# A four-layer hybrid encoder on one core: the first round of each MLP in a new order

## The chip, the cores and the metric

The kernel runs on one core of a Trainium2 chip. The metric is the device time of one execution in microseconds (us), the median of several runs. Five engines work side by side and wait for each other by semaphores: PE (TensorE, matmuls), ACT (ScalarE), DVE (VectorE), POOL (GpSimd) and SP (SyncE, which here issues the loads of weights).

## The reference

Four layers over 512 tokens of width 1024. Each layer adds a token mixer (latent attention, a gated recurrence, or windowed attention) and then an MLP:

```
x = x + mixer(rmsnorm(x, norm_mix[i]))
x = x + square(relu(rmsnorm(x, norm_mlp[i]) @ w1[i])) @ w2[i]      # 1024 -> 4096 -> 1024
```

with rmsnorm(x, g) = x * rsqrt(mean(x*x) + 1e-6) * g, and one more rmsnorm at the end. All in float32. The change is in the MLPs, of which there are four.

## The kernel before

**Precision.** Every float32 operand is split in two parts, a rounded high part and the remainder, and a product is three matmuls: high by high, low by high, high by low (L674 to L676). ACT rounds (a copy into w_hi, h_hi or u_hi), DVE subtracts (w_lo, h_lo, u_lo). `split(n)` on ACT (L2400) and on DVE (L1479) does this for the next n weight units of 128x1024. There are four slots for split weights, so ACT may round unit n when PE has done with unit n - 4.

**The MLP.** It runs in four slices of 1024 of the 4096 hidden features. A slice has two groups (g = 0, 1) of 512 features, and then the down projection of the slice, `down(0)` and `down(1)`: 8 units of 24 matmuls with 512 columns. A group is one round of `seven_products`: a fast matrix product of 2x2 blocks with seven block products (24 matmuls of 256 columns each) in place of eight. Its weights are sums of blocks of w1, in this order:

- product 1: A11; product 2: A11+A21; product 3: A11+A21+A22; product 4: A12; product 5: A21+A22; product 6: A22; product 7: A11+A12+A21+A22.

DVE makes each sum in place, just after its w_lo of an earlier unit (L1485, L1489, L1492, L1496). L1496 makes the weights of product 7; ACT's rounding of them waits for it by `sums_made`. On the other side stand the token halves H11, H21, H22 and their sums T1 to T4, which are made once per MLP in b11, b12, b21, b22; these four lie in the places that the second half of u_hi and u_lo takes later.

**One round on the other engines.** Between the products ACT and DVE combine results in c11, c21, c12, c22 (the buffer called relu): ACT copies a bank after product 1 (c11, L2527; product 3 waits for this copy), after product 3 (c21, L2536; product 5 waits) and the other bank (c22, L2539; product 6 waits). DVE adds after product 4 (L1707), subtracts after product 5 (c22, L1711; product 7 waits for this by `c_added`) and after product 6 (c21, L1714). Then ACT takes relu, squares and rounds (u_hi, L2518), DVE makes u_lo (L1687). A round of group 1 finds the results of group 0 still in c12 and c22: `u_lo_of(0, 1)` on DVE must be done before ACT overwrites c22.

**The first group of each MLP** is done differently, by plain products of four units (`square_group`), whose last quarter follows the two matmuls of `norm_sums` (L758, L760). It needs no sums of tokens, and while it runs ACT and DVE make T1 to T4. Its result stands in two PSUM areas. ACT takes the relu of area 0, then of area 1 (L2465), both into the buffer relu, DVE squares (L1611), ACT rounds (L2471), DVE makes the remainder (L1617). The c11 of the first round overwrites area 0's part of that buffer. Between these stand the root of the norm on ACT (a table load and L2447) and var on DVE (L1547). Down waits for both remainders by `u_ready`.

Each engine does its list in the order in which it is written; nothing is reordered.

Of the kernel before, what the change touches and what calls it, by code (L numbers as in the profile page):

```python
# [22 lines left out]
ALU = mybir.AluOpType  # L23
# [9 lines left out]
KC = D // P  # L33
# [119 lines left out]
def weight_plan():  # L153

    raws, ops, raw_starts = [], [], []
    sums = 0
# [110 lines left out]
def trunk(nc, A):  # L267
    raws, ops, raw_starts = weight_plan()
    with ExitStack() as ctx:
# [1175 lines left out]
        def _(dve):  # L1445
# [16 lines left out]
            def split(n):  # L1462

                for _ in range(n):
# [78 lines left out]
            def norm_var():  # L1543

                sum_ready()
                root_ready()
# [59 lines left out]
            def squares_of(q):  # L1606

                c.add(f"area{q}")
                dve.wait_ge(area_free[q], c.now(f"area{q}"))
                r = chunk(mlp_m["relu"], 2 * q, 2)  # L1610
                nc.vector.tensor_tensor(r, r, r, ALU.mult).then_inc(squared, 1)  # L1611

            def low_of_squares(q):

                c.add("u_hi")
                dve.wait_ge(u_hi_done, c.now("u_hi"))
                nc.vector.tensor_tensor(chunk(u_lo, 2 * q, 2), chunk(mlp_m["relu"], 2 * q, 2),  # L1617
                                        exact(chunk(u_hi, 2 * q, 2)), ALU.subtract).then_inc(u_ready, 1)

            def add_scaled(g):  # L1620

# [68 lines left out]
            def seven_products(g):  # L1690
# [3 lines left out]
                c.add("rounds")  # L1694
                c.add("tensor_unit", 3)
                split(1)
                if r % 7 == 0:
                    nc.vector.tensor_tensor(b21, b21, b11, ALU.add).then_inc(turned_made, 1)
                split(1)
                if r % 7 == 0:  # L1700
                    turned_lo(T4, b21)
                elif g == 1:
                    u_lo_of(0, 1)
                split(1)
                product_passed()
# [12 lines left out]
                split(1)  # L1718
                c.add(f"area{xy}")

            def mlp(gain):
# [14 lines left out]
                squares_of(0)  # L1736
                split(1)
                low_of_squares(0)
                norm_var()
                squares_of(1)  # L1740
                split(1)
                low_of_squares(1)
                c.add("psum_done")
                c.add("tensor_unit", 4)
                for s in range(SLICES):
                    if s:
                        seven_products(0)
                    seven_products(1)
# [620 lines left out]
        def _(act):  # L2369
# [89 lines left out]
            def relu_of(q):  # L2459

                if q == 0:
                    act.wait_ge(psum_done, c.now("psum_done") + 2)
                else:
                    units_passed(4)
                nc.scalar.activation(chunk(mlp_m["relu"], 2 * q, 2), area(q), ACT.Relu).then_inc(area_free[q], 1)  # L2465

            def high_of_squares(q):

                c.add("squared")
                act.wait_ge(squared, c.now("squared"))  # L2470
                nc.scalar.activation(chunk(u_hi, 2 * q, 2), chunk(mlp_m["relu"], 2 * q, 2), ACT.Copy  # L2471
                                     ).then_inc(u_hi_done, 1)

            def down_passed():
# [45 lines left out]
            def seven_products(g):  # L2520
# [8 lines left out]
                if r % 7 == 0:  # L2529
                    turned_hi(T4, b21)  # L2530
                elif g == 1:
                    u_hi_of(0, 1)
                split(1)
                product_passed()
# [17 lines left out]
                act.wait_ge(area_free[xy], jobs["round", r][0])  # L2552
                c.add("u_ready", 2)

            def half_gained(n, ks):

                for k in ks:
# [2 lines left out]
                                         ).then_inc(gained_done, 1)  # L2560

            def mlp(n, gain):
                half_gained(n - 1, range(4 if PHASES[n - 1][0] == "mla" else 0, KC))
                split(1)
                turned_hi(T1, b11)
                sums_hi()
# [12 lines left out]
                for s in range(SLICES):  # L2579
                    if s:  # L2580
                        seven_products(0)
                    seven_products(1)
                    u_hi_of(1, 1)
                    if s + 1 == SLICES:
                        break
# [641 lines left out]
```

## Time and profile before

| | us |
|---|---|
| median of 3 runs | 2027.55 (2026.84 to 2027.86) |
| profiled execution: its time | 2027.66 |
| profiled execution: its span, first to last instruction | 2025.8 |
| PE busy / DVE busy / ACT busy | 2000.3 / 1432.3 / 1063.8 |
| granted clock of PE, mean | 0.997 |

PE is busy for 99% of the span, so the time is what PE has to do, plus the stretches in which PE waits or runs at a lower clock. The time of an execution lies 1.9 us above its span. The timeline gives, for each instruction, its start and its duration; where instructions of an engine overlap in its pipeline the distance of two starts is what one costs. In brackets behind a row stands the idle time before it and what ended it.

### The profile page before, as it was taken

What the parts mean: (1) busy time and instruction counts of PE and PEld (TensorE: products, weight loads), DVE (VectorE), ACT (ScalarE), POOL (GpSimd) and SP (SyncE); (2) the same over time, 40 slices, a digit from 0 to 9 for tenths busy, and PEclk for the clock granted to TensorE, in tenths of its full rate; (3) what the DMA queues carried; (4) which work ended last, traced back from release to release, by engine and by line L of the source; (5) the groups of instructions that cost most, each with busy time, mean ns of one, the idle gap of its engine ahead of it and who ended that gap; (6) DMA issues with size and microseconds to landing.
All of it is one profiled execution on the core that took longest, in us unless ns stands there. A gap on an engine that the chain in (4) does not pass through costs nothing.

```text
span 2025.8 us, 28746 instructions
## 1 busy us (share of the span) xinstructions
PE 2000.3 (99%) x11760; PEld 1748.8 (86%) x11760; DVE 1432.3 (71%) x1682; ACT 1063.8 (53%) x1508; POOL 247.3 (12%) x323
## 2 busy tenths in 40 slices
PE   9999999999999999999999999999999999999998
PEld 8888898989878789899888888898988888899897
DVE  7866865756897867567698786675787758667574
ACT  6655534625466646254456663553647646353453
POOL 7002000000200200002731200000641011000000
PEclk9999999999999999999999999999999999999999
DMA  6222324314223133241332242422422223242431
GB/s 193 61 68 78 120 64 125 113 57 143 86 81 103 64 125 115 61 148 57 119 89 70 61 138 84 125 84 83 148 76 71 59 67 122 66 146 63 125 115 42
DMA packets 152595, 193.20 MB, mean 95 GB/s; under 512 B 17712, under 2 KB 95088, under 8 KB 152464
## 3 DMA queue, kind: packets, MB, share of 16 engines
q1 hardware_dynamic: 145520, 186.04, 29.6%
q0 software_dynamic: 4544, 3.94, 0.7%
q8 instruction: 93, 1.52, 0.3%
q10 hardware_dynamic: 2400, 1.38, 0.2%
q14 instruction: 38, 0.31, 0.1%
HBM read 185.30 MB, written 2.10 MB: 93 GB/s over the span
## 4 chain that ended last, share of the span: by engine, by line
PE 89%; DVE 6%; POOL 2%; ACT 2%; DMA 1%; issue 1%; ACTq 0%; DVEq 0%; POOLq 0%; SPq 0%
PE psum L674 27%; PE psum L676 27%; PE psum L675 27%; DVE h_lo L1514 2%; PE psum L1113 2%; PE psum L1086 1%; DVE w_lo L1479 1%; DMA arena<-in_mlp_w 1%; PE psum L1221 1%; DVE arena_r L1675 1%; PE psum L1062 1%; PE psum L1058 1%; PE psum L1057 1%; PE psum L1063 0%; DVE arena L1611 0%
## 5 line engine op out<-in xcount | busy, mean ns | idle before, releaser
L1479 DVE TENSOR_TENSOR w_lo<-w_raw,w_hi 128x1024 fp32r<-128x1024 f32 (+1 forms) x303 | 374.5, 1240 | 239.5 <-ACT w_hi L2400 238.3
L2400 ACT ACTIVATE w_hi<-w_raw 128x1024 fp32r<-128x1024 f32 (+1 forms) x307 | 323.6, 1060 | 328.3 <-PE psum L676 292.7
L674 PE MATMUL psum<-u_hi,w_hi 128*128 128x512 f32 x1256 | 492.2, 392 | 0.1
L676 PE MATMUL psum<-u_hi,w_lo 128*128 128x512 f32 x1256 | 489.1, 389 | 0.0
L675 PE MATMUL psum<-u_lo,w_hi 128*128 128x512 f32 x1256 | 489.1, 389 | 0.0
L674 PE MATMUL psum<-h_hi,w_hi 128*128 128x256 f32 (+1 forms) x1368 | 440.4, 322 | 0.0
L675 PE MATMUL psum<-h_lo,w_hi 128*128 128x256 f32 (+1 forms) x1368 | 437.5, 320 | 0.0
L676 PE MATMUL psum<-h_hi,w_lo 128*128 128x256 f32 (+1 forms) x1368 | 437.3, 320 | 0.0
L676 PEld LDWEIGHTS psum<-u_hi,w_lo 128*128 128x128 f32 x1256 | 235.8, 188 | 49.6
L674 PEld LDWEIGHTS psum<-u_hi,w_hi 128*128 128x128 f32 x1256 | 235.9, 188 | 49.0 <-DVE u_lo L1809 1.2
L674 PEld LDWEIGHTS psum<-h_hi,w_hi 128*128 128x128 f32 x1368 | 260.3, 190 | 20.2 <-issue 1.1
L2400 ACT ACTIVATE w_hi<-arena 128x1024 fp32r<-128x1024 f32 x120 | 127.1, 1060 | 286.5 <-PE psum L676 256.2
L675 PEld LDWEIGHTS psum<-h_lo,w_hi 128*128 128x128 f32 x1368 | 260.6, 190 | 19.3 <-issue 1.0
L675 PEld LDWEIGHTS psum<-u_lo,w_hi 128*128 128x128 f32 x1256 | 236.0, 188 | 47.4
L676 PEld LDWEIGHTS psum<-h_hi,w_lo 128*128 128x128 f32 x1368 | 260.5, 190 | 18.9
L1479 DVE TENSOR_TENSOR w_lo<-arena,w_hi 128x1024 fp32r<-128x1024 f32 x120 | 146.9, 1224 | 166.6 <-ACT w_hi L2400 166.2
L674 PE MATMUL psum<-arena_r,w_hi 128*128 128x256 f32 x672 | 191.0, 284 | 12.0 <-ACT arena L2527 11.0
L676 PE MATMUL psum<-arena_r,w_lo 128*128 128x256 f32 x672 | 190.8, 284 | 0.0
L675 PE MATMUL psum<-arena_r,w_hi 128*128 128x256 f32 x672 | 188.9, 281 | 0.0
L3067 POOL TENSOR_TENSOR ssq<-ssq,sq 128x512 f32<-128x512 f32 x49 | 80.2, 1636 | 685.4 <-ACT sq L2436 683.2
L674 PEld LDWEIGHTS psum<-arena_r,w_hi 128*128 128x128 f32 x672 | 128.6, 191 | 13.1 <-ACT arena L2527 11.8
L675 PEld LDWEIGHTS psum<-arena_r,w_hi 128*128 128x128 f32 x672 | 128.7, 191 | 0.0
(333 smaller groups left out, 2589.3 us busy)
## 6 DMA issues: line engine op xcount, KB each, us to landing
w_raw<-in_mlp_w SPq DMA_DIRECT2D x176, 512.0 KB, 3.9
arena<-in_mlp_w SPq DMA_DIRECT2D x80, 512.0 KB, 4.9
w_raw<-in_mla_w_o SPq DMA_DIRECT2D x16, 512.0 KB, 3.8
w_raw<-in_lru_w_in SPq DMA_DIRECT2D x16, 512.0 KB, 3.9
w_raw<-in_swa_w_in SPq DMA_DIRECT2D x12, 512.0 KB, 4.2
w_raw<-in_mla_w_ukv SPq DMA_DIRECT2D x8, 512.0 KB, 4.7
w_raw<-in_lru_w_out SPq DMA_DIRECT2D x8, 512.0 KB, 3.6
w_raw<-in_swa_w_o SPq DMA_DIRECT2D x8, 512.0 KB, 4.0
```

The source lines that it names most:

```text
L674: nc.tensor.matmul(out, stat[0], mov[0], start=start, stop=False, skip_group_check=skip)
L675: nc.tensor.matmul(out, stat[0], mov[1], start=False, stop=False, skip_group_check=skip)
L676: return nc.tensor.matmul(out, stat[1], mov[0], start=False, stop=stop, skip_group_check=skip)
L1057: nc.tensor.matmul(out, qh, KLO[s][:, 0:keys_n], start=False, stop=False)
L1058: nc.tensor.matmul(out, ql, KHI[s][:, 0:keys_n], start=False, stop=False)
L1062: nc.tensor.matmul(out, ROPE_Q[s][:, q_at], ROPE_KHI[:, 0:keys_n], start=False, stop=False)
L1086: mm = nc.tensor.transpose(area(a)[:, at:at + P], mla_m["p"][:, S_OFF[b] + P * jt:S_OFF[b] + P * (jt + 1)], ident)
L1113: mm = nc.tensor.matmul(bank(3, 1)[:, P * jt:T], mla_m["v"][:, v_at:v_at + VD], mla_m["pt"][:, T_OFF[jt]:T_OFF[jt] + n], start=jt == 0, st ...
L1479: ins = nc.vector.tensor_tensor(w_lo[:, to], tile, exact(w_hi[:, to]), ALU.subtract)
L1514: nc.vector.scalar_tensor_tensor(out=low, in0=rows, scalar=col(*gain(k)), in1=exact(high), op0=ALU.mult, op1=ALU.subtract).then_inc(h_read ...
L2400: nc.scalar.activation(w_hi[:, to], raw_tile(op.raw), ACT.Copy).then_inc(w_hi_done, 1)
L3067: g.tensor_tensor(to, to, source, ALU.add).then_inc(squares_added, 1)
```

## The change

1. In `weight_plan` and DVE's `split`, the sum for product 7 is made behind the w_lo of A22 (product 6) in place of the w_lo of A21+A22 (product 5). This holds for all 28 rounds.
2. The relu and squares of area 1 of the first group go to the place of b12 in place of the buffer relu, so the first round's c-buffers wait for area 0's part alone; ACT waits there for T3 (`turned_ready`).
3. A new `first_round` on DVE and ACT replaces `seven_products(1)` for the first round of each MLP. Root and var come late in it, and the square, rounding and remainder of area 1 come after the subtraction of product 6. ACT's copies of products stand ahead of roundings of weights, or closer to the product they wait for.
4. The rounding and remainder of the norm's sums (`sums_hi`, `sums_lo`) come earlier, and `norm_var` waits for the root in another place.

```diff
@@ weight_plan: seven()
-        ops.append(Operand("A21+A22", q, (b, a), made=sums + 3))
+        ops.append(Operand("A21+A22", q, made=sums + 3))
         q.freed = len(ops)
-        ops.append(Operand("A22", e))
+        ops.append(Operand("A22", e, (b, a)))
@@
+        first_squares_at = by_chunk(first_tokens), b12
@@ DVE: split()
-                    elif op.role == "A21+A22":
+                    elif op.role == "A22":
                         b, a = op.others
                         nc.vector.tensor_tensor(raw_tile(b), raw_tile(b), raw_tile(a), ALU.add).then_inc(sums_made, 1)
@@ DVE
+            def first_round(r):
...
+                split(2)
+                nc.vector.tensor_tensor(b21, b21, b11, ALU.add).then_inc(turned_made, 1)
+                split(1)
+                turned_lo(T4, b21)
+                product_passed()
+                dve.wait_ge(c_copied, 3 * r + 1)
+                nc.vector.tensor_tensor(c11, bank(2, 1), c11, ALU.add).then_inc(c_added, 1)
+                split(1)
+                product_passed()
+                dve.wait_ge(c_copied, 3 * r + 3)
+                nc.vector.tensor_tensor(c22, c22, bank(2, 0), ALU.subtract).then_inc(c_added, 1)
+                root_ready()
+                norm_var()
+                c.add("psum_done")
+                product_passed()
+                free(nc.vector.tensor_tensor(c21, bank(3, 0), c21, ALU.subtract), 3)
+                squares_of(1)
+                split(1)
+                low_of_squares(1)
+                split(1)
+                u_lo_of(1, 0)
...
@@ DVE: mlp()
                 nc.vector.tensor_tensor(b11, b11, b12, ALU.subtract).then_inc(turned_made, 1)
+                sums_lo()
...
                 turned_lo(T1, b11)
-                sums_lo()
                 turned_lo(T3, b12)
...
                 low_of_squares(0)
-                norm_var()
-                squares_of(1)
-                split(1)
-                low_of_squares(1)
-                c.add("psum_done")
@@ ACT
+            def first_round(r):
...
+                nc.scalar.activation(c11, bank(2, 0), ACT.Copy).then_inc(c_copied, 1)
+                split(2)
+                product_passed()
+                product_passed()
+                nc.scalar.activation(c21, bank(2, 0), ACT.Copy).then_inc(c_copied, 1)
+                split(1)
+                turned_hi(T4, b21)
+                need(act, x_ready, c.now("x_ready"))
+                nc.scalar.activation(c22, bank(3, 0), ACT.Copy).then_inc(c_copied, 1)
+                c.add("tensor_unit", 3)
+                split(1)
+                norm_root(bank(3, 1))
...
+                act.wait_ge(c_added, 2 * r + 2)
+                link(nc.scalar.activation(c22, c22, ACT.Relu))
+                split(1)
+                high_of_squares(1)
...
@@ ACT: mlp()
                 high_of_squares(0)
+                act.wait_ge(turned_ready, 4 * (c.now("turned") // 4) + 2)
                 relu_of(1)
-                norm_root(bank(3, 1))
-                c.add("psum_done")
-                split(1)
-                high_of_squares(1)
```

The instructions of PE and of SP stand as before, with the same waits. The places below are where rows move.

DVE in the second and later slices of an MLP, in the round of group 1: w_lo of products 5 and 6, the sum for product 7, the remainder of group 0's second half, w_lo of product 7, then the additions of the round. Before:

```order
L1479 TENSOR_TENSOR w_lo<-w_raw,w_hi 128x1024 x2
L1496 TENSOR_TENSOR w_raw<-w_raw 128x1024
L1479 TENSOR_TENSOR w_lo<-w_raw,w_hi 128x1024
L1687 TENSOR_TENSOR u_lo<-arena,u_hi 128x4x256
L1479 TENSOR_TENSOR w_lo<-w_raw,w_hi 128x1024
L1707 TENSOR_TENSOR arena<-psum,arena 128x512
L1479 TENSOR_TENSOR w_lo<-arena,w_hi 128x1024
L1711 TENSOR_TENSOR arena<-arena,psum 128x512
```

And in the changed kernel:

```order
L1481 TENSOR_TENSOR w_lo<-w_raw,w_hi 128x1024 x3
L1498 TENSOR_TENSOR w_raw<-w_raw 128x1024
L1688 TENSOR_TENSOR u_lo<-arena,u_hi 128x4x256
L1481 TENSOR_TENSOR w_lo<-w_raw,w_hi 128x1024
L1704 TENSOR_TENSOR arena<-psum,arena 128x512
L1481 TENSOR_TENSOR w_lo<-arena,w_hi 128x1024
L1708 TENSOR_TENSOR arena<-arena,psum 128x512
```

The sum stands one w_lo later, directly ahead of the remainder (L1687, now L1688).

DVE in the first round of an MLP, from the remainder of area 0's squares on. Before (L1611 and L1617 are square and remainder of area 1):

```order
L1617 TENSOR_TENSOR u_lo<-arena,u_hi 128x1024
L1547 TENSOR_SCALAR var<-psum 128x512
L1611 TENSOR_TENSOR arena<-arena 128x1024
L1479 TENSOR_TENSOR w_lo<-w_raw,w_hi 128x1024
L1617 TENSOR_TENSOR u_lo<-arena,u_hi 128x1024
```

In the changed kernel the end of the same round (L1732 is the subtraction of product 5, L1737 that of product 6):

```order
L1732 TENSOR_TENSOR arena<-arena,psum 128x512
L1548 TENSOR_SCALAR var<-psum 128x512
L1737 TENSOR_TENSOR arena<-psum,arena 128x512
L1612 TENSOR_TENSOR u_hi_f<-u_hi_f 128x4x256
L1481 TENSOR_TENSOR w_lo<-w_raw,w_hi 128x1024
L1618 TENSOR_TENSOR u_lo<-u_hi_f,u_hi 128x1024
```

Square and remainder of area 1 moved from ahead of the round to behind its sixth product.

## Rows read from the trace of the kernel before

**Rows 1.** Waits of PE: who waited for whom, us in total, times, longest us.

```profile
PE psum L674 <- ACT arena L2527: 11.0, 4, 2.8
PE psum L760 <- DVE sq_r L1533: 4.8, 5, 1.3
```

**Rows 2.** Timeline, PE: start us, us, what; first sum and first down matmul of four MLPs.

```profile
202.81 0.39 PE L758 MATMUL psum<-sq_r,ones_r 128*128 128x512 f32 x1
...
234.34 0.40 PE L674 MATMUL psum<-u_hi,w_hi 128*128 128x512 f32 x1
...
690.20 0.39 PE L758 MATMUL psum<-sq_r,ones_r 128*128 128x512 f32 x1
...
722.23 0.40 PE L674 MATMUL psum<-u_hi,w_hi 128*128 128x512 f32 x1
...
1170.06 0.39 PE L758 MATMUL psum<-sq_r,ones_r 128*128 128x512 f32 x1
...
1201.67 0.40 PE L674 MATMUL psum<-u_hi,w_hi 128*128 128x512 f32 x1
...
1689.34 0.39 PE L758 MATMUL psum<-sq_r,ones_r 128*128 128x512 f32 x1
...
1721.13 0.40 PE L674 MATMUL psum<-u_hi,w_hi 128*128 128x512 f32 x1
```

**Rows 3.** Timeline, PE: last quarter of a group; two rounds of slice 2, first MLP.

```profile
204.46 0.40 PE L674 MATMUL psum<-h_hi,w_hi 128*128 128x512 f32 x1
...
209.92 0.28 PE L674 MATMUL psum<-h_hi,w_hi 128*128 128x256 f32 x1
...
277.89 0.28 PE L674 MATMUL psum<-h_hi,w_hi 128*128 128x256 f32 x1
...
317.88 0.40 PE L674 MATMUL psum<-u_hi,w_hi 128*128 128x512 f32 x1
```

**Rows 4.** Windows, PE: stretch, its us, busy us (instructions), granted clock, DMA share, GB/s.

```profile
218.50:221.50 3.00, 2.93 (x13) 0.50 0.00 0
1192.90:1194.90 2.00, 1.92 (x16) 1.00 0.03 8
```

**Rows 5.** Timeline, PE: product 5 of the third MLP's first round, behind a wait.

```profile
1192.98 0.39 PE L674 MATMUL psum<-arena_r,w_hi 128*128 128x256 f32 x1 [1.03 <-ACT arena L2536]
1193.21 0.28 PE L675 MATMUL psum<-arena_r,w_hi 128*128 128x256 f32 x1
```

**Rows 6.** Timeline, DVE: remainder of the norm's sums; of the first squares (two MLPs).

```profile
203.38 0.68 DVE L1533 TENSOR_TENSOR sq_r<-ssq,sq_r 128x512 fp32r<-128x512 f32 x1
203.99 1.22 DVE L1675 TENSOR_TENSOR arena_r<-u_hi_f,arena_r 128x1024 fp32r<-128x1024 f32 x1
...
213.07 1.22 DVE L1617 TENSOR_TENSOR u_lo<-arena,u_hi 128x1024 fp32r<-128x1024 f32 x1
...
700.80 1.22 DVE L1617 TENSOR_TENSOR u_lo<-arena,u_hi 128x1024 fp32r<-128x1024 f32 x1
```

**Rows 7.** Timeline, ACT: four instructions in the two rounds of Rows 3.

```profile
280.96 0.60 ACT L2527 ACTIVATE arena<-psum 128x512 f32<-128x512 f32 x1 [1.75 <-PE psum L676]
...
287.81 1.06 ACT L2400 ACTIVATE w_hi<-arena 128x1024 fp32r<-128x1024 f32 x1
...
302.15 0.60 ACT L2527 ACTIVATE arena<-psum 128x512 f32<-128x512 f32 x1
...
309.11 0.60 ACT L2539 ACTIVATE arena<-psum 128x512 f32<-128x512 f32 x1 [1.83 <-DVE u_lo L1687]
```

**Rows 8.** Timeline, DVE: six instructions in the same two rounds.

```profile
286.56 1.22 DVE L1496 TENSOR_TENSOR arena<-arena 128x1024 f32<-128x1024 f32 x1
...
288.90 1.23 DVE L1479 TENSOR_TENSOR w_lo<-arena,w_hi 128x1024 fp32r<-128x1024 f32 x1
...
300.81 1.23 DVE L1687 TENSOR_TENSOR u_lo<-arena,u_hi 128x1024 fp32r<-128x1024 f32 x1 [0.77 <-ACT u_hi L2518]
...
306.71 1.23 DVE L1479 TENSOR_TENSOR w_lo<-w_raw,w_hi 128x1024 fp32r<-128x1024 f32 x1 [0.62 <-ACT w_hi L2400]
...
310.69 1.23 DVE L1479 TENSOR_TENSOR w_lo<-w_raw,w_hi 128x1024 fp32r<-128x1024 f32 x1 [1.61 <-ACT w_hi L2400]
...
313.56 0.68 DVE L1711 TENSOR_TENSOR arena<-arena,psum 128x512 f32<-128x512 f32 x1
```

More of the change, by code:

```diff
@@ L1545, in norm_var @@
                 sum_ready()
-                root_ready()
                 link(nc.vector.tensor_scalar(var[:, :], bank(3, 1), 1.0 / D, EPS, ALU.mult, ALU.add))
@@ L1609, in squares_of @@
                 dve.wait_ge(area_free[q], c.now(f"area{q}"))
-                r = chunk(mlp_m["relu"], 2 * q, 2)
+                r = first_squares_at[q]
                 nc.vector.tensor_tensor(r, r, r, ALU.mult).then_inc(squared, 1)
@@ L1616, in low_of_squares @@
                 dve.wait_ge(u_hi_done, c.now("u_hi"))
-                nc.vector.tensor_tensor(chunk(u_lo, 2 * q, 2), chunk(mlp_m["relu"], 2 * q, 2),
-                                        exact(chunk(u_hi, 2 * q, 2)), ALU.subtract).then_inc(u_ready, 1)
+                nc.vector.tensor_tensor(by_chunk(chunk(u_lo, 2 * q, 2)), first_squares_at[q],
+                                        exact(by_chunk(chunk(u_hi, 2 * q, 2))), ALU.subtract).then_inc(u_ready, 1)
             def add_scaled(g):
@@ L1696, in seven_products @@
                 split(1)
-                if r % 7 == 0:
-                    nc.vector.tensor_tensor(b21, b21, b11, ALU.add).then_inc(turned_made, 1)
                 split(1)
-                if r % 7 == 0:
-                    turned_lo(T4, b21)
-                elif g == 1:
+                if g == 1:
                     u_lo_of(0, 1)
@@ L1719, in seven_products @@
                 c.add(f"area{xy}")
+            def first_round(r):
+                c.add("rounds")
+                c.add("tensor_unit", 3)
[21 more added lines that the diff above has]
+                split(1)
+                c.add("tensor_unit")
+                split(1)
+                c.add("area2")
             def mlp(gain):
@@ L1747, in mlp @@
                         seven_products(0)
-                    seven_products(1)
+                        seven_products(1)
+                    else:
+                        first_round(c.now("rounds"))
                     u_lo_of(1, 1)
@@ L2464, in relu_of @@
                     units_passed(4)
-                nc.scalar.activation(chunk(mlp_m["relu"], 2 * q, 2), area(q), ACT.Relu).then_inc(area_free[q], 1)
+                nc.scalar.activation(first_squares_at[q], by_chunk(area(q)), ACT.Relu).then_inc(area_free[q], 1)
             def high_of_squares(q):
@@ L2470, in high_of_squares @@
                 act.wait_ge(squared, c.now("squared"))
-                nc.scalar.activation(chunk(u_hi, 2 * q, 2), chunk(mlp_m["relu"], 2 * q, 2), ACT.Copy
+                nc.scalar.activation(by_chunk(chunk(u_hi, 2 * q, 2)), first_squares_at[q], ACT.Copy
                                      ).then_inc(u_hi_done, 1)
@@ L2528, in seven_products @@
                 split(1)
-                if r % 7 == 0:
-                    turned_hi(T4, b21)
-                elif g == 1:
+                if g == 1:
                     u_hi_of(0, 1)
@@ L2553, in seven_products @@
                 c.add("u_ready", 2)
+            def first_round(r):
+                c.add("rounds")
+                product_passed()
+                act.wait_ge(u_ready, c.now("u_ready") - 1)
+                nc.scalar.activation(c11, bank(2, 0), ACT.Copy).then_inc(c_copied, 1)
+                split(2)
+                product_passed()
+                product_passed()
+                nc.scalar.activation(c21, bank(2, 0), ACT.Copy).then_inc(c_copied, 1)
[3 more added lines that the diff above has]
+                nc.scalar.activation(c22, bank(3, 0), ACT.Copy).then_inc(c_copied, 1)
+                c.add("tensor_unit", 3)
+                split(1)
+                norm_root(bank(3, 1))
+                c.add("psum_done")
+                act.wait_ge(c_added, 2 * r + 2)
+                link(nc.scalar.activation(c22, c22, ACT.Relu))
+                split(1)
+                high_of_squares(1)
+                act.wait_ge(area_free[3], jobs["round", r][1])
+                split(1)
+                link(nc.scalar.activation(first_tokens, first_tokens, ACT.Relu))
+                act.wait_ge(u_ready, c.now("u_ready"))
+                u_hi_of(1, 0)
+                split(1)
+                product_passed()
+                nc.scalar.activation(c12, bank(2, 0), ACT.Relu).then_inc(area_free[2], 1)
+                split(1)
+                act.wait_ge(area_free[2], jobs["round", r][0])
+                c.add("u_ready", 2)
             def half_gained(n, ks):
@@ L2562, in mlp @@
             def mlp(n, gain):
-                half_gained(n - 1, range(4 if PHASES[n - 1][0] == "mla" else 0, KC))
+                if PHASES[n - 1][0] != "mla":
+                    half_gained(n - 1, range(4))
+                    sums_hi()
+                    half_gained(n - 1, range(4, KC))
+                else:
+                    half_gained(n - 1, range(4, KC))
+                    sums_hi()
                 split(1)
                 turned_hi(T1, b11)
-                sums_hi()
                 turned_hi(T3, b12)
@@ L2581, in mlp @@
                         seven_products(0)
-                    seven_products(1)
+                        seven_products(1)
+                    else:
+                        first_round(c.now("rounds"))
                     u_hi_of(1, 1)
```

## The prediction

> **What bounds the kernel now.** I read the shares of the page first, in the table above: PE is busy for 99% of the span, so only what PE waits for, or does at a low clock, can be won, and anything that delays PE costs at once. The list of PE's waits comes next [rows 1]: product 3 waits 11.0 us, once in each of the four MLPs, for ACT's copy c11; L760 waits 4.8 us, of which four of the five waits (4.3 us) are in the MLPs, for the remainder of the norm's sums; one copy of c21 costs 1.0 us, at product 5 of the third MLP [rows 5]. All lie in one stretch, from the first sum matmul of an MLP to its first down matmul. No wait of PE stands in any later round.
>
> The length of that stretch says what the waits cost with their after-effects [rows 2]: 31.53, 32.03, 31.61 and 31.79 us, together 126.96. Without waits it would be the last quarter of the group, 209.92 - 204.46 = 5.46, two sum matmuls (2/24 of that, 0.45), and one round: two rounds take 317.88 - 277.89 = 39.99, so one takes 20.00 and one product 2.86 [rows 3]. That makes 25.91. Over it stand 5.62, 6.12, 5.70 and 5.88 us, **23.3 us in all**. The named waits are 16.4 of it. Most of the rest is clock: after the wait in the first MLP PE's granted clock is 0.50 (1.2 GHz, of 2.4) for 3 us, in which it does 13 matmuls and not some 25 [rows 4]; the second and the fourth MLP show the same, the third does not. Some 13 matmuls that take 0.23 in place of 0.12 us cost 1.4 us, so about 4 us in all. The last part is the restart: the matmul behind a wait is followed after 0.23 us [rows 5], in a flow after 2.86 / 24 = 0.12, so 0.11 is lost. From one engine to the next some 0.03 to 0.05 passes: ACT's start at 287.81 [rows 7] stands 0.03 behind the end of the sum at 286.56 [rows 8]. I use both below, 0.05 for PE.
>
> **First stretch, what goes.** The norm's sums are rounded and their remainder taken before ACT and DVE turn to the weights, which come late by DMA. So the wait of L760 goes: about 1.1 to 1.5 us a time. What is late next is c11, which needs the remainder of area 0's squares on DVE. That one starts at 213.07 [rows 6] at the end of a queue without gaps; with the norm remainder (0.6 from its start, 203.38, to the next, 203.99) gone from the queue it starts at 212.47 and ends at 213.69. The copy follows at once, since root, table load, area 1's rounding and a rounding of weights are no longer ahead of it: 213.72 to 214.30. PE, which did not wait at L760, is due at product 3 at 202.81 + 0.45 + 5.46 + 2 x 2.86 = 214.44. It waits for nothing, or some hundredths. In the second MLP the remainder starts at 700.80 [rows 6], less 0.60, plus 0.6 for the rounding of the sums that now stands among ACT's eight scalings of tokens, for which DVE waits there; the copy ends at 702.62, due is 690.20 + 11.63 = 701.83: a wait of 0.8 + 0.05 + 0.11. In the third some 0.15, in the fourth none. Sum: **1.1 us** left of the waits at product 3.
>
> **First stretch, what comes.** Down now waits for the remainder of area 1, which stands behind the subtraction of product 6. From the end of product 6, at t: DVE starts the subtraction at t + 0.2, as ACT's copy c11 at 280.96 [rows 7] follows the end of product 1 (277.89 + 2.86 = 280.75); the square comes 0.60 later; then ACT's rounding of it (1.06) runs beside a w_lo (1.14), and the remainder starts at t + 3.1 and ends at t + 4.35. Product 7 ends at t + 2.86. So PE waits 1.53, and 0.11 with the restart: 1.64 x 4 = **6.6 us**. The durations are those of the same shapes in rows 7 and 8. The other deadlines in the round hold by my count: weights for product 4 by 0.7 us, T4 for product 6 by 0.3, the subtraction for product 7 by 0.8.
>
> So 1.1 + 6.6 = 7.7 us stay of 23.3: the first stretches give back **15.6 us**. This assumes that a wait of 1.5 us does not bring the low clock.
>
> **The later slices.** The moved sum acts in all rounds, also where nothing was waiting. The pair of rounds from 277.89 on stands for 12 such pairs (slices 2 to 4 of four MLPs). I follow the queues of DVE and ACT.
>
> Group 0: the sum at 286.56 [rows 8] goes behind the next w_lo and starts at 287.69, and ends at 288.91. ACT's rounding for product 7 at 287.81 [rows 7] started 0.03 after the sum's end; now 288.94. Its w_lo, 288.90, becomes 290.03, so +1.13. From there DVE's queue is full, and where it has a gap it waits for an ACT rounding that waits for a DVE sum, so the delay stays. The subtraction for product 7 still comes in time, at 294.74 for 295.00. But the remainder at 300.81 becomes 301.93 and ends at 303.16; the copy c11 of the next round, 302.15, waited for it and starts at 303.26, ends at 303.86. Product 3 is due at 277.89 + 9 x 2.857 = 303.60. PE waits 0.31 and restarts for 0.11: **0.42**.
>
> Group 1: before, the sum lay in a hole of DVE, ahead of the w_lo at 306.71 that waited for ACT. Now it stands behind that w_lo, which itself is at 307.85, so the remainder L1687 starts not at 307.86 but at 310.12, and ends at 311.35. ACT's copy c22, 309.11, waited for it [rows 7]: 311.38, +2.27. The rounding behind it and the w_lo at 310.69 [rows 8] move by the same, as that gap was a wait for ACT; and then the subtraction at 313.56 becomes 315.83 to 316.52. Product 7 was due at 317.88 - 2.86 = 315.02, with the 0.42 at 315.44. PE starts at 316.57: 1.13, and 0.11: **1.25**. The slack that was there, 315.02 - 314.24 = 0.8, is used up. After product 7 nothing more is late: u_lo must be ready at the third down unit, 10.9 us on, and was ready after some 6.3.
>
> Sum: 1.67 us a pair, x 12 = **20.0 us**. Bounds: if only one of the two delays reaches the subtraction, PE waits 315.38 + 0.05 - 315.02 + 0.11 = 0.52, or 6 us over all pairs; if the slack counts for nothing, 2.3 us, or 27 us.
>
> **The rest at nothing:** DMA. Loads for the freed slots are issued up to 2.3 us later, and are wanted over 3 us after they landed; PE's and SP's own lists are unchanged.
>
> **The sum.** 2025.8 - 15.6 + 20.0 = 2030.2 us of span; the profiled execution took 1.9 more than its span and 0.1 more than the median, so the median becomes 2027.55 + 4.4 = **2032.0 us**. Two large terms nearly cancel.
>
> **The rivals.**
> A. The moved sum is hidden in the later slices, by work I put in series that is not. For it: DVE is busy 1432.3 us of 2025.8, and the holes at 306.71 and 310.69 (0.62, 1.61) lie right there [rows 8]. Against: each of these holes is a wait for ACT, which in turn waits for DVE. It gives 2027.55 - 15.6 = 2012.0. Chance 0.08.
> B. One of the two delays is absorbed: 6 us lost, 2018. Chance 0.07.
> C. The low clock comes with the new waits: slower still. At half clock as in rows 4 each costs 1.4 us more: four at down give 2037.6, twelve more at product 7 give 2054. For: the waits of 2.75 us brought it three times in four. Against: the wait of 1.0 us before 1192.98 was followed by a granted clock of 1.00 [rows 4, 5]. [...] The Trainium skill, "TensorE: Matmul & The Clock Gate", section "What's actually happening", has the array fall from 2.4 to 1.2 GHz when it was idle, which three of the four long waits agree with. Chance 0.06.
> D. The first stretch does not do what is said: c11 stays late since DVE's queue, not ACT's, holds it. If PE lost 1 us more in each MLP, 2036. It is in my range. Chance 0.07, with the part of C that lies there.
> The forecast itself, 2027 to 2037, has the remaining 0.72.
>
> **How the numbers follow.** A measurement can tell about 0.2%, 4.05 us: faster is below 2023.5, slower above 2031.6. The forecast lies at that edge. Its size rests on 12 like pairs: 0.1 us a pair is 1.2 us, so about 0.42 of its 0.72 falls above the edge and 0.30 below. Slower: 0.42 + 0.06 + 0.04 = 0.52; faster: A and B, 0.15; same: 0.33. For 8 in 10 I take 2024 to 2039: the forecast, D, and the smaller part of C.
>
> **What would show it.** In the changed kernel's trace: no wait at L760 in the MLPs; at product 3 of a first round only the second MLP with some 0.8 us; PE waiting 1.5 us at the first down matmul for a u_lo four times; and in each later pair a wait of about 1.1 us at product 7 for DVE's subtraction (12 times) and about 0.3 at product 3 for c11. A pair of rounds would take 41.7 us and not 40.0. If there is no wait at product 7, A is right; if it is below 0.5 us, B. A granted clock under 1 behind a wait of 1.1 or 1.5 us shows C.

## The result, and the profile after

| | before | changed |
|---|---|---|
| median of 6 runs each, us | 2027.22 (2026.30 to 2027.86) | 2034.52 (2033.85 to 2035.08) |
| ratio to before, 95% interval | | 1.0036 (1.0023 to 1.0049) |
| profiled execution: time / span, us | 2027.66 / 2025.8 | 2033.85 / 2032.1 |
| first stretches of the four MLPs, us | 126.96 | 111.58 |
| the 12 pairs of rounds, us | 479.9 | 501.4 |

The change costs 7.3 us, 0.36%. The forecast was 2032.0, 4.4 above its base of 2027.55, with a range of 2024 to 2039; "slower by over 0.2%" had the largest chance. "First stretch" is from the first sum matmul of an MLP to its first down matmul, and a "pair" is the two rounds of a slice, from the first matmul of group 0 to the first down matmul, both as in the prediction.

The shares hardly move. The page of the changed kernel:

```profile
span 2032.1 us, 28751 instructions
PE 2000.7 (98%) x11760; PEld 1746.2 (86%) x11760; DVE 1431.6 (70%) x1682; ACT 1060.7 (52%) x1508; POOL 243.1 (12%) x323
```

Every engine is as busy as before within 5 us, and the span is 6.3 us longer: the time is in waits. PE's waits in the changed kernel (who waited for whom: us in total, times, longest), which answer to [rows 1]:

```profile
PE psum L676 <- DVE arena L1708: 12.1, 12, 1.2
PE psum L676 <- DVE u_lo L1618: 6.2, 4, 1.6
PE psum L676 <- ACT arena L2551: 3.2, 12, 0.7
...
PE psum L676 <- ACT arena L2582: 0.8, 1, 0.8
PE psum L762 <- DVE sq_r L1535: 0.5, 1, 0.5
```

The two lines of [rows 1] are gone from the MLPs: of L674's waits for c11, 2.7 to 2.8 us in all four, 0.8 us is left in the second MLP (L2582, the copy c11 of the first round), and of L760's five none. (The 0.5 us at L762, at 1512.93, is in no MLP; it was the fifth.) The first and third line are the later slices: twelve waits at product 7 for DVE's subtraction, and twelve at product 3 for the copy c11 (L2551, once L2527). The second line is the new one at the first down matmul, four times.

The first stretch of the first and of the second MLP, timeline of PE (start, duration, what; in brackets the idle time before and its releaser), which answers to the first four of [rows 2]:

```profile
202.54 0.39 PE L760 MATMUL psum<-sq_r,ones_r 128*128 128x512 f32 x1
...
230.14 0.47 PE L676 MATMUL psum<-u_hi,w_hi 128*128 128x512 f32 x1 [1.56 <-DVE u_lo L1618]
...
691.09 0.39 PE L760 MATMUL psum<-sq_r,ones_r 128*128 128x512 f32 x1
...
719.77 0.47 PE L676 MATMUL psum<-u_hi,w_hi 128*128 128x512 f32 x1 [1.55 <-DVE u_lo L1618]
```

230.14 - 202.54 = 27.60 where it was 31.53, and 28.68 where it was 32.03; the other two take 27.70 and 27.60. Over the 25.91 without waits stand 1.69, 2.77, 1.79 and 1.69. (In the third MLP c11 comes just in time, and the 0.10 is the restart alone.)

A pair of rounds, slice 2 of the first MLP, timeline of PE, which answers to the last two of [rows 3]:

```profile
273.78 0.28 PE L676 MATMUL psum<-h_hi,w_hi 128*128 128x256 f32 x1
...
299.81 0.39 PE L676 MATMUL psum<-arena_r,w_hi 128*128 128x256 f32 x1 [0.16 <-ACT arena L2551]
...
312.44 0.39 PE L676 MATMUL psum<-h_hi,w_hi 128*128 128x256 f32 x1 [0.96 <-DVE arena L1708]
...
315.42 0.40 PE L676 MATMUL psum<-u_hi,w_hi 128*128 128x512 f32 x1
```

315.42 - 273.78 = 41.64 where it was 39.99. The 1.65 are the two waits and their restarts. The bracket gives less than the delay, since it counts from the modelled end of the matmul before (0.28 from its start, where the next one in a flow starts after 0.12). From start to start the steps over 0.12 are these: 299.81 stands 0.44 behind its predecessor, so 0.32 late, and its successor another 0.10 to 0.11; 312.44 stands 1.24 behind, so 1.12 late, and its successor 0.11. Together 1.65. Behind the second wait, on DVE (timeline):

```profile
303.73 1.23 DVE L1481 TENSOR_TENSOR w_lo<-w_raw,w_hi 128x1024 fp32r<-128x1024 f32 x1 [1.76 <-ACT w_hi L2424]
304.87 1.22 DVE L1498 TENSOR_TENSOR w_raw<-w_raw 128x1024 f32<-128x1024 f32 x1
306.00 1.22 DVE L1688 TENSOR_TENSOR u_lo<-arena,u_hi 128x1024 fp32r<-128x1024 f32 x1
308.83 1.23 DVE L1481 TENSOR_TENSOR w_lo<-w_raw,w_hi 128x1024 fp32r<-128x1024 f32 x1 [1.61 <-ACT w_hi L2424]
...
311.71 0.68 DVE L1708 TENSOR_TENSOR arena<-arena,psum 128x512 f32<-128x512 f32 x1
```

and on ACT, the copy c22, which answers to the last of [rows 7]:

```profile
307.26 0.60 ACT L2561 ACTIVATE arena<-psum 128x512 f32<-128x512 f32 x1 [3.08 <-DVE u_lo L1688]
```

ACT idles 3.08 us ahead of c22, where it idled 1.83: c22 waits for the remainder L1688, which now stands behind a w_lo and the sum. And DVE idles 1.61 us ahead of the w_lo at 308.83, as it did at 310.69 in [rows 8]: that hole did not shrink, since it is a wait for ACT. The hole that did vanish is the other one, the 0.62 at 306.71, out of which the sum was taken; there is now one hole of 1.76 where the sum of 1.13 and the hole of 0.62 were. So DVE is idle for 30% of the span, and the delay goes through all the same.

Ten of the twelve pairs take 41.63 to 41.65 us. Two take 42.50: the last slices of the second and of the third MLP. The one of the second MLP, timeline of PE:

```profile
933.77 0.28 PE L676 MATMUL psum<-h_hi,w_hi 128*128 128x256 f32 x1
...
976.27 0.40 PE L676 MATMUL psum<-u_hi,w_hi 128*128 128x512 f32 x1
```

The experiments turn to these too.

### The profile page after: what moved, and what is told of

Read it like the earlier page. It is cut to its first block, busy times and chain, and to the rows that moved or that the text cites. A ratio compares the mean times of both kernels' runs of the same rounds, so it can differ in the third digit from the quotient of the medians.

```text
span 2032.1 us, 28751 instructions
## 1 busy us (share of the span) xinstructions
PE 2000.7 (98%) x11760; PEld 1746.2 (86%) x11760; DVE 1431.6 (70%) x1682; ACT 1060.7 (52%) x1508; POOL 243.1 (12%) x323
## 4 chain that ended last, share of the span: by engine, by line
PE 83%; DVE 9%; ACT 4%; issue 2%; POOL 2%; DMA 0%; DVEq 0%; ACTq 0%; POOLq 0%
PE psum L676 26%; PE psum L678 25%; PE psum L677 25%; DVE w_lo L1481 3%; ACT w_hi L2424 2%; PE psum L1115 2%; DVE h_lo L1516 1%; PE psum L1088 1%; DVE u_lo L1688 1%; PE psum L1223 1%; DVE w_raw L1498 1%; ACT arena L2541 1%; PE psum L1064 1%; PE psum L1060 1%; PE psum L1059 1%
## 5 line engine op out<-in xcount | busy, mean ns | idle before, releaser
L1481 DVE TENSOR_TENSOR w_lo<-w_raw,w_hi 128x1024 fp32r<-128x1024 f32 (+1 forms) x303 | 373.4, 1239 | 244.3 <-ACT w_hi L2424 241.8
L2424 ACT ACTIVATE w_hi<-arena 128x1024 fp32r<-128x1024 f32 x120 | 126.1, 1058 | 282.4 <-PE psum L678 240.2
L1481 DVE TENSOR_TENSOR w_lo<-arena,w_hi 128x1024 fp32r<-128x1024 f32 x120 | 146.9, 1224 | 169.1 <-ACT w_hi L2424 168.6
L676 PEld LDWEIGHTS psum<-arena_r,w_hi 128*128 128x128 f32 x672 | 126.5, 188 | 6.7 <-ACT arena L2551 5.6
L677 PEld LDWEIGHTS psum<-arena_r,w_hi 128*128 128x128 f32 x672 | 126.6, 188 | 0.0
```

Source lines behind the costliest of these rows:

```text
L676: nc.tensor.matmul(out, stat[0], mov[0], start=start, stop=False, skip_group_check=skip)
L677: nc.tensor.matmul(out, stat[0], mov[1], start=False, stop=False, skip_group_check=skip)
L1481: ins = nc.vector.tensor_tensor(w_lo[:, to], tile, exact(w_hi[:, to]), ALU.subtract)
L2424: nc.scalar.activation(w_hi[:, to], raw_tile(op.raw), ACT.Copy).then_inc(w_hi_done, 1)
```

## The experiments

Two theories of why the sum costs time in the later slices, and two of the two odd pairs, had to be told apart; the last runs try what the first ones point to. In the diffs the base is named ahead.

**1. The new order without the moved sum.** Base: the changed kernel.

```diff
-        ops.append(Operand("A21+A22", q, made=sums + 3))
+        ops.append(Operand("A21+A22", q, (b, a), made=sums + 3))
         q.freed = len(ops)
-        ops.append(Operand("A22", e, (b, a)))
+        ops.append(Operand("A22", e))
...
-                    elif op.role == "A22":
+                    elif op.role == "A21+A22":
```

> The changed kernel with the sum for product 7 back behind the w_lo of product 5; all else of the change stays. My theory (the change is two parts: the first stretches win 15.4 us, the moved sum loses 19.8 us in twelve pairs of rounds, and 1.7 more in the two pairs beside which POOL works): a pair takes 40.0 us, no wait of PE at product 7, a median of about 2012. Rival (the first rounds' new order itself makes later rounds late, or both parts need each other): the later waits stay at least in part, median above 2020.

Measured: 2012.87 us (2012.69 to 2013.50) beside 2027.96; ratio 0.9926 (0.9911 to 0.9941). First stretches 27.98, 28.70, 27.69 and 27.64, together 112.0; all twelve pairs 39.99 to 40.00. PE's waits:

```profile
PE psum L676 <- DVE u_lo L1618: 6.2, 4, 1.6
PE psum L676 <- DVE w_lo L1481: 1.1, 1, 1.1
...
PE psum L676 <- ACT arena L2582: 0.8, 1, 0.8
```

The lines of L1708 and L2551 are gone, those of the first stretch (L1618, L2582) are as in the changed kernel. So the new order alone is worth 15 us, and the whole loss of the later slices hangs on the place of one sum. (The 1.1 us for L1481 is once, at 13.14, in the first phase. A wait of 0.6 to 1.5 us stands there in the profiled run of every experiment and in neither of those of before and changed. It hangs on the load of x: ACT's rounding of x that this load releases starts at 8.22 us before and at 7.89 in the changed kernel, and at 8.38 to 9.55 in the eight experiments, though the instructions up to there are the same. I leave it out of the comparison.)

**2. The moved sum alone.** Base: the kernel before, with the reverse of the diff above.

> The kernel before with only the sum for product 7 moved behind the w_lo of product 6. My theory: a pair of rounds takes 41.65 us, two pairs 42.5, so 21.5 us more; in the first rounds it lets ACT copy c21 1 us earlier, which takes away the one wait of 1.0 us at product 5. Median about 2047.5. Rival (the moved sum costs only together with the new first round): 2027 to 2030.

Measured: 2048.86 us (2047.49 to 2049.74) beside 2027.96; ratio 1.0102 (1.0087 to 1.0117). Ten pairs 41.62 to 41.65, two 42.50, together 501.4 as in the changed kernel; first stretches 126.1 for 126.96 before.

```profile
PE psum L674 <- ACT arena L2527: 14.2, 16, 2.8
PE psum L674 <- DVE arena L1711: 12.9, 14, 1.2
```

The two halves of the change act apart from each other. The pairs cost 21.5 us with either order of the first round. In the first rounds the sum costs nothing in the new order (112.0 without it, 111.6 with it); in the old one two of them get a wait of 0.41 us at product 7 (14 times, not 12), but the wait of 1.0 us at product 5 of the third MLP goes, as expected, and in this execution the granted clock falls behind two of the four long waits and not three, which gives back 1.4. By medians the parts are -15.1 and +20.9, together +5.8, and the whole is +7.3; the interval of each ratio is 3 us to either side, so the medians can't tell the two from each other. By stretches and pairs they are -15.0 and +20.6, together +5.6, and the whole +6.1; the 0.5 between them is less than that chance of the clock.

**3 and 4. The sum late in one group only.** Base: the kernel before; `late` is `(at // T) % 2 == 0` for group 0 in the first kernel, `== 1` for group 1 in the second. The prediction traced two delays, one in each group, and took them as in series with one slack of 0.8 us.

```diff
+        late = (at // T) % 2 == 0
-        ops.append(Operand("A21+A22", q, (b, a), made=sums + 3))
+        ops.append(Operand("A21+A22", q, () if late else (b, a), made=sums + 3))
...
-        ops.append(Operand("A22", e))
+        ops.append(Operand("A22", e, (b, a) if late else ()))
...
-                    elif op.role == "A21+A22":
+                    elif op.role in ("A21+A22", "A22") and op.others:
```

> The kernel before with the sum late only in rounds of group 0. My theory (two delays of 1.13 us in series, against a slack of 0.8 at product 7): this one delay reaches product 3 of the next round with 0.4 us and is then covered by that shift at product 7, so 0.45 us a pair, 12 pairs 5.4 us, one more for the two pairs beside POOL: about 2033.5. Rival (each delay has half of the loss): 0.8 us a pair, 2037.

> The kernel before with the sum late only in rounds of group 1. My theory: no wait at product 3; product 7 waits 0.35 to 0.4 us, 0.5 with the restart, 12 pairs 6 us, one more for the two pairs beside POOL, 1.2 less for the c21 wait of the third MLP: about 2033. Rival (the hole of DVE at that place hides it): 2026 to 2027. Rival (half of the loss each): 2036.

Measured: group 0 2036.65 us (2035.49 to 2037.35), ratio 1.0042 (1.0027 to 1.0057), ten pairs of about 40.50 and two of 41.62; group 1 2034.36 us (2033.38 to 2036.05), ratio 1.0032 (1.0020 to 1.0043), ten pairs of about 40.51, one of 40.70 and one of 40.91. PE's waits, group 0 first:

```profile
PE psum L675 <- ACT arena L2528: 14.2, 16, 2.8
...
PE psum L675 <- DVE arena L1712: 0.8, 2, 0.4
```

```profile
PE psum L675 <- ACT arena L2528: 11.1, 4, 2.8
...
PE psum L675 <- DVE arena L1712: 3.8, 12, 0.7
```

L2528 is L2527 of before and L1712 is L1711, both one line lower. Group 0 alone gives the wait at product 3 (14.2 - 11.0 = 3.2 us in the twelve pairs) and none at product 7 except in two pairs; group 1 alone gives none at product 3 and 0.3 us at product 7 in most. So the step holds: each delay by itself is partly swallowed by a slack of 0.8 us, and both together cost 1.65 a pair, which is not 0.51 + 0.52 = 1.03. Group 0's delay meets a slack of its own first, ahead of product 3 (c11 was ready at 302.75 for 303.60), and costs 0.32 there and 0.10 for the restart; what is left of it reaches product 7 in time but for another restart of 0.10. Group 1's alone costs 0.43 and a restart, the 0.52 that the prediction has as its lower bound. The size that I expected of group 0 was missed, 2036.65 for 2033.5. Of the 3.2 us some 1.2 are the two odd pairs (1.63 each, where I had given both together 1 us over the others), 0.7 are the 0.51 a pair in place of 0.45, and 0.8 are the base, which lay at 2027.96 in these runs. In the kernel with group 1 alone the granted clock fell behind all four long waits.

**5 and 6. The two odd pairs.** In both, POOL works beside DVE. It makes the rotary tables of the next mixer as soon as the positions are there. Timeline of POOL in the changed kernel, its first table instruction and two instructions of one shape:

```profile
949.49 0.68 POOL L3163 CAST arena<-arena 128x128 f32<-128x128 int32 x1 [264.56 <-DMA arena<-in_positions]
...
951.11 0.46 POOL L3167 TENSOR_TENSOR arena<-arena 128x128 f32<-128x128 f32 x1
951.65 1.32 POOL L3168 TENSOR_TENSOR arena<-arena 128x128 f32<-128x128 f32 x1
```

and DVE beside it, where the same shapes took 1.23 and 1.22 in the pair of the first MLP:

```profile
951.14 1.51 DVE L1481 TENSOR_TENSOR w_lo<-w_raw,w_hi 128x1024 fp32r<-128x1024 f32 x1 [0.53 <-ACT w_hi L2424]
952.58 1.48 DVE L1491 TENSOR_TENSOR w_raw<-w_raw 128x1024 f32<-128x1024 f32 x1
...
956.52 1.48 DVE L1494 TENSOR_TENSOR w_raw<-w_raw 128x1024 f32<-128x1024 f32 x1
```

Theory: both engines slow each other, in the kernel before too, where there is slack for it. Rival: something else of the last slice (the next phase's loads, its first instructions, or the loads of the positions that delay weights). Test: move the load of the positions, four weight units later in one kernel, sixteen earlier in the other, and the slow pairs must go or move. Base: the changed kernel.

```diff
                 if kind == "mlp":
-                    load_until(end - 8)
+                    load_until(end - 4)
                     if before_rotary(n):
```

> The changed kernel, but the loads of positions, which start POOL's work on the rotary tables, are issued four weight loads later, so POOL starts some 22 us later, behind most of the pair of rounds. My theory (POOL's work lengthens DVE's instructions from 1.22 to as much as 1.5 us, and the chain of DVE and ACT has no slack left in the changed kernel, so these two pairs take 42.5 and not 41.65 us): both pairs take 41.7, median 1.7 us less, 2032.8. Rival (those two pairs are late through DMA: the loads of positions delay weights): the same gain, but w_lo rows of DVE stay at 1.3 to 1.5 us beside no POOL work. Rival (neither): 2034.5.

Measured: 2037.23 us (2035.89 to 2038.88), ratio 1.0047 (1.0032 to 1.0062). POOL starts at 970.09, and all twelve pairs take 41.61 to 41.64, together 499.6 in place of 501.4. Groups of DVE by form, window of 949.5 to 973 (busy us, mean ns; idle before), in the changed kernel and then in this one:

```profile
L1481 DVE TENSOR_TENSOR w_lo<-w_raw,w_hi 128x1024 fp32r<-128x1024 f32 x6 | 7.9, 1319 | 4.8 <-ACT w_hi L2424 4.8
...
L1494 DVE TENSOR_TENSOR w_raw<-w_raw 128x1024 f32<-128x1024 f32 x1 | 1.5, 1481 | 0.0
```

```profile
L1481 DVE TENSOR_TENSOR w_lo<-w_raw,w_hi 128x1024 fp32r<-128x1024 f32 x6 | 7.4, 1226 | 4.9 <-ACT w_hi L2424 4.9
...
L1494 DVE TENSOR_TENSOR w_raw<-w_raw 128x1024 f32<-128x1024 f32 x1 | 1.2, 1216 | 0.0
```

With POOL away the two rows of DVE are back at 1.23 and 1.22 us; by the rival of the loads they would have stayed long. That settles the two pairs. It gained nothing as a whole, though: what POOL does late is late in the next phase. Timeline of PE in the window-attention layer, and the window behind it (its us, PE busy, PEld, DVE, ACT, POOL, granted clock, DMA share, GB/s):

```profile
1032.20 0.47 PE L760 MATMUL psum<-sq_r,ones_r 128*128 128x512 f32 x1 [1.27 <-ACT sq_r L2466]
...
1033.73 0.50 PE L762 MATMUL psum<-sq_r,ones_r 128*128 128x512 f32 x1 [1.07 <-DVE sq_r L1535]
```

```profile
1035.00:1038.00 3.00, 3.00 (x13) 2.71 (x12) 2.89 (x3) 0.94 (x2) 0.00 (x0) 0.50 0.89 244
```

What is late there begins 20 us earlier. POOL's timeline, and then ACT's:

```profile
996.95 15.85 POOL L3200 DMA_DIRECT2D arena<-arena  x32 [0.30 <-POOL arena L3194]
1012.82 4.06 POOL L3127 TENSOR_TENSOR ssq<-ssq,sq 128x512 f32<-128x512 f32 x3
```

```profile
1014.15 0.63 ACT L2460 ACTIVATE sq<-x 128x512 f32<-128x512 f32 x1 [7.00 <-POOL ssq L3127]
```

POOL issues the copies of the finished tables until 1012.80 and only then takes up the norm's sums of squares, which it had begun at 1005.52 in the changed kernel. ACT waits 7.0 us for them, and the last of the next such sums starts at 1029.79 where it was 1027.22. Some 4 us are lost by two waits close together and 3 us at 1.2 GHz behind them. The changed kernel has no wait of PE there. Against the 1.8 us that the two pairs give back stand also 0.6 more at L762 in a later phase and the wait of 1.5 us near 13 us. The two waits at 1032.20 and 1033.73 are the one place in the ten profiled runs where the clock fell behind waits of this size.

The other kernel has the load of the positions sixteen units earlier:

```diff
                 if kind == "mlp":
-                    load_until(end - 8)
+                    load_until(end - 24)
                     if before_rotary(n):
                         load_positions(sp, pos_loaded)
+                    load_until(end - 8)
```

> The changed kernel with the loads of positions issued sixteen weight loads earlier, so that POOL makes the rotary tables beside a down projection and not beside the last pair of rounds of the second and third MLP. (Four loads later made these pairs 41.6 us, but the tables then came late and cost more elsewhere.) My theory (POOL's work slows DVE, and only the pairs have no slack): all pairs 41.65, no new wait at the next phase, median 1.7 us below the changed kernel, 2032.8. Rival (POOL's work costs about the same wherever it stands): 2034.5.

Measured: 2034.87 us (2034.54 to 2035.16), ratio 1.0035 (1.0022 to 1.0049): no gain. POOL starts at 864.42, and the slow pairs, 42.55 us each, are now the ones before, the pair from 849 to 892 us and its like in the third MLP; the last slices take 41.65. My new place was another pair of rounds, not a place without one. As a saving it failed; as a test of the cause it says the same as the run above: the slow pair goes where POOL's tables go.

**7. The new order, sum back, and the squares of area 1 early.** The first run leaves the wait at down, 6.2 us in four. In the changed kernel DVE has a hole of 1.67 us in the first round, while PE does products 2 and 3 (timeline):

```profile
211.67 1.22 DVE L1618 TENSOR_TENSOR u_lo<-arena,u_hi 128x1024 fp32r<-128x1024 f32 x1
214.56 1.23 DVE L1481 TENSOR_TENSOR w_lo<-w_raw,w_hi 128x1024 fp32r<-128x1024 f32 x1 [1.67 <-ACT w_hi L2424]
```

The square of area 1 (1.13 from start to start) fits there, and its rounding and remainder can then come ahead of product 6. Base: the kernel of the first run.

```diff
@@ DVE first_round
+                squares_of(1)
                 split(2)
...
                 root_ready()
+                low_of_squares(1)
                 norm_var()
...
-                squares_of(1)
-                split(1)
-                low_of_squares(1)
-                split(1)
+                split(2)
@@ ACT first_round
                 nc.scalar.activation(c11, bank(2, 0), ACT.Copy).then_inc(c_copied, 1)
                 split(2)
+                high_of_squares(1)
...
-                high_of_squares(1)
```

> The kernel of e1_sum_back with area 1's squares earlier in the first round: the square on DVE straight behind the remainder of area 0, where DVE waits 1.7 us for a rounding; its rounding on ACT ahead of the copy c21; its remainder behind the subtraction of product 5. My theory (the wait of 1.55 us at the first down matmul comes from that chain standing behind product 6): the wait goes, 1.65 us four times, so 6.6 us less than e1: about 2005.5. Rival (the instructions moved ahead make product 4, 6 or 7 late instead): the first stretches stay at 27.6 us, 2012 or more.

Measured: 2006.05 us (2005.84 to 2006.32), ratio 0.9893 (0.9877 to 0.9910). First stretches 25.86, 26.97, 26.32 and 26.48; the waits at down are gone, and what is left is c11 in three MLPs:

```profile
PE psum L676 <- ACT arena L2581: 1.3, 3, 0.8
```

The remainder of area 1 stands at 224.33, ahead of the subtraction of product 6 and no longer behind it. From the first run the first stretches fall by 112.0 - 105.6 = 6.4 us, against 4 x 1.69 = 6.8 that stood at down; in the third and fourth MLP c11, which had waited for nothing, comes 0.4 to 0.6 us late in exchange.

**8. And the remainder of area 0 ahead of a sum.** c11 waits for that remainder, which stands behind the sum A21+A22 for product 5. Base: the kernel above; on DVE the two change places. `sum_later` makes `split` leave that sum out, and `sum_of_last` makes it.

```diff
...
-                split(1)
+                split(1, sum_later=True)
                 low_of_squares(0)
+                sum_of_last()
```

> The kernel of e5_early_squares, and in the first round the remainder of area 0's squares ahead of the sum for product 5 on DVE, so ahead by 1.13 us; the copy c11 follows it. My theory (what is left of the wait at product 3, 1.3 us in three MLPs, hangs on this place in DVE's queue alone): no wait at product 3, 1.3 us and three restarts of 0.1 less, median 1.5 us below e5, 2004.5. Rival (the sum, now later, makes the weights of product 5 late): 2006 or more.

Measured: 2004.71 us (2004.53 to 2005.27), ratio 0.9887 (0.9874 to 0.9901). First stretches 25.89, 26.00, 25.89 and 25.88, together 103.66, for 4 x 25.91 = 103.64 without waits; pairs 479.9. All of PE's waits of 0.3 us and more:

```profile
PE psum L676 <- DVE w_lo L1487: 1.2, 1, 1.2
PE psum L1432 <- POOL ones L3210: 1.0, 1, 1.0
PE psum L762 <- DVE sq_r L1541: 0.4, 1, 0.4
PE psum L1341 <- DVE arena L2313: 0.3, 1, 0.3
```

None of these lies in an MLP. This version is 22.7 us faster than the kernel before the change (2027.45 in the same runs) and, by medians of different runs, 29.8 faster than the changed one.

## Why the prediction was right, and where it was off

- **What bounds the kernel, and the 25.91 us without waits.** Shown: the last kernel's first stretches come to 103.66 for 103.64, with no wait left in them.
- **First stretch, what goes and comes.** The forecast was 15.6 us back; measured 15.4. Some of that is chance: the low clock, 1.4 us each time, came behind three of the four long waits in the profile of before, and behind two, three and four of them in those of the second, third and fourth experiment. No wait at L760 (now L762) in the MLPs. The wait for c11 is 0.8 us in the second MLP, forecast 0.8 + 0.05, and a restart of 0.10 in the third, forecast 0.15. At down PE is 1.69 us late, forecast 1.53: in the first MLP u_lo ends at 228.76 + 1.23 = 229.99 and PE starts at 230.14, 0.15 behind it and not 0.05. The 0.11 of the restart lies behind the stretch's end.
- **The later slices.** The pair of rounds was forecast at 41.67 us and is 41.64 in ten of twelve: 0.32 + 0.11 at product 3 (forecast 0.31 + 0.11) and 1.12 + 0.11 at product 7 (forecast 1.13 + 0.11). The delays behind them stand as forecast: the sum behind the w_lo, L1688 behind the sum, ACT's idle time ahead of c22 longer by 1.25 (forecast 2.27 - 1.13 = 1.14), the hole of 1.61 unshrunk. The runs with one group alone show that the two delays add up at product 7 and share its slack.
- **The mis-sized term.** "The pair of rounds from 277.89 on stands for 12 such pairs" holds for ten. Two cost 2.50 in place of 1.67, so the term is 21.5 us and not 20.0. The sign of it was in the trace of before, in rows that I did not weigh: there, too, DVE's sums beside POOL take longer, and the slack of 0.8 us hid it. From the timeline of DVE before:

```profile
953.87 1.49 DVE L1492 TENSOR_TENSOR w_raw<-w_raw 128x1024 f32<-128x1024 f32 x1
```

  Before, that pair took 40.00 like all others. A change that uses up a slack also uncovers what the slack had covered; I priced the slack in the quiet pair and multiplied by 12.
- **The sum.** By spans: -15.4 + 21.5 = +6.1 of the 6.3 seen, forecast +4.4; the two odd pairs are 2 x (2.50 - 1.65) = 1.7 of what was missing. The medians differ by 7.3 because the profiled execution of before lay 0.4 above its median and that of the changed kernel 0.7 below its own.
- **The rivals.** A (the sum hidden) and B (one delay absorbed) are out: PE is late at product 7 twelve times, by 1.12 us or more, where A had nothing and B less than 0.5. The price of B was right, and the runs with one delay show it, 0.51 and 0.52 a pair. C (low clock) did not come: behind the wait of 1.56 at down the granted clock is 1.00, where [rows 4] had 0.50 behind 2.75. D (c11 late because of DVE's queue) is 0.8 us in one MLP, as in the forecast.

The clock behind the new wait at down, window of the changed kernel (columns as above):

```profile
230.20:233.20 3.00, 3.00 (x13) 2.45 (x14) 1.28 (x2) 2.94 (x4) 0.00 (x0) 1.00 0.75 228
```

The 13 matmuls in these 3 us have 512 columns, those of [rows 4] 256, so the same count is twice the work. The Trainium skill, "TensorE: Matmul & The Clock Gate", section "What's actually happening", has the array fall to 1.2 GHz when it idled; the waits of 1.0 to 1.6 us here did not bring that, except for the two close together in the fifth experiment. Nor does the length of a single wait settle it: in the second experiment waits of 2.74 us were followed by 0.50 in the first MLP and by 1.00 in the second.

What stays open: why the load of x lands later in the profiled executions of the experiments, and what decides whether the clock falls behind a wait; no run was made for either.

## What to carry to other kernels

An engine that is 30% idle is not free where its holes are waits for a partner that waits for it: an instruction moved out of the hole into the ring delays both, and each round pays. Read the holes by their releaser before moving anything, and when an edit to a shared helper serves a special first round, count the rounds in which nothing was wrong; here the special rounds gained 15 us and the 12 ordinary pairs lost 21.5. Slack is to be priced in the worst of the like places, not in the one that the trace shows first, and of delays that share one slack only the first is covered by it (0.51 and 0.52 alone, 1.65 together).

## What of the hardware was not expected

- **POOL's elementwise work lengthens DVE's, and DVE's lengthens POOL's.** Of DVE's 128x1024 instructions with both operands in SBUF some go from 1.22 to as much as 1.51 us while POOL runs 128x128 ones, and of those some go from 0.46 to 1.32. In none of the ten traces does one of them take over 1.23 or 0.47 us while the other engine is idle. DVE's 128x512 instructions that read PSUM stayed at 0.68. The Trainium skill, "GPSIMD Engine Reference", section "1. Specifications", says that its SBUF interfaces are shared with VectorE, with contention for DVE instructions that have two SBUF inputs; the traces agree, and these are the sizes.
- **Short waits did not lower the clock, two together once did.** Four waits of 1.55 us and twelve of 0.96 to 1.25 in the changed kernel left the granted clock at 1.00 in the 4 us behind each of them; waits of 1.27 and 1.07 us within 1.6 us were followed by 3 us at 0.50, as single ones of 2.73 to 2.79 were in twelve of sixteen cases, those of before and of the second to fourth experiment together.
